# A hybrid diffusion backbone on one core: filler products behind the level batches, and state sums with 64 weight columns

## The chip, the cores and the metric

The kernel runs on one core of one Trainium2 chip. The metric is the device time of one execution in microseconds (us), the median of the runs shown. TensorE runs at one of two clocks, 1.2 or 2.4 GHz; the profile gives the granted share, 0.50 or 1.00.

## The reference, cut to what matters

One trunk layer runs over 256 context and 2048 latent tokens of width 1024: modulation, one input projection, two recurrences, an output projection and an MLP. The change lies in the second recurrence, HGRN2, 8 heads of 64, forward and backward:

```python
def step(s, xs):
    q_c, k_c, v_c, b_c, qd_c, kd_c, fl_c = xs
    diff = b_c[:, :, :, None, :] - b_c[:, :, None, :, :]
    dec = masked_exp(diff, incl)
    a = jnp.einsum('bhid,bhjd,bhijd->bhij', q_c, k_c, dec)
    o = jnp.einsum('bhck,bhkv->bhcv', qd_c, s) + jnp.einsum('bhij,bhjv->bhiv', a, v_c)
    s = fl_c[..., None] * s + jnp.einsum('bhck,bhcv->bhkv', kd_c, v_c)
    return s, o
```

Inside a chunk the attention `a` of a pair (i, j) carries the product of the decays between j and i; the sum over `kd_c` and `v_c` is what the chunk adds to the state.

## The kernel before, in words

The program is a row of phases: front, projection, the first recurrence, a short context phase, the chunk stage (`phase_hgrn_chunks`, line 1764), a phase that scans the states, and the output phases with the MLP. The change touches the chunk stage alone.

The chunk stage works on chunks of C2 = 128 tokens, 16 in all, as 8 periods `j` of two lanes `g` (0 and 1). Partitions 0 to 63 hold the forward direction, 64 to 127 the backward one. The decayed attention is built by doubling: at level `l` (0 to 6) blocks of `1 << l` tokens are joined. For each level and lane:

- TensorE makes a level batch (`level`, lines 2052 and 2053; 32 products, 64 records in the trace, 64 rows by 64 weight columns and 32 moving columns, which fall on the four quarters of the array in turn). Level 6 is `across` (lines 2064 and 2065, two quarters).
- VectorE copies the blocks by mask into `am` (`attend`, 2289) and multiplies the queries by the decay (2309). GpSimd multiplies the keys (2248) and, once per level, makes the next decay products `gg` (`products`, 2229). ScalarE copies half of the keys for the backward side (2162). All of these release the same lane's next level batch.

Between the level batches TensorE's program has other steps of the periods before and after: `tail` (transposes of the keys, 2075 and 2076) at levels 0 and 2, `sums` at levels 1 and 3, `head` (value transposes 2024 and first products 2032) of period j + 1 at levels 4 and 5. `sums` has two parts: the attention times the values (2094, through `values`), and the state sums (2107): for each of 8 heads one product with a 128 by 128 weight tile of `kdt`, whose 128 columns are the two directions of 64, and 64 moving columns. ScalarE evicts the first part; VectorE copies the second into `delta` (2316).

The order on each engine is the order of the loops in its own `body`; TensorE's is unrolled over all periods. At the end of a period ScalarE copies the level 6 result (`b_ax`, 2165) behind its key copy, which waits for GpSimd's level 6; only then may TensorE begin level 0 of the next period. SyncE's queue prefetches with waits on `level_done`. Ahead of the stage `warm_up` issues ten full-array products of constants with 384 columns (2115).

Of the kernel before, what the change touches and what calls it, by code (L numbers as in the profile page):

```python
# [1763 lines left out]
def phase_hgrn_chunks(nc, e):  # L1764

    with nc.cleanup_on_exit(), ExitStack() as ctx:
# [3 lines left out]
        def sem(n):  # L1770
            return nc.alloc_semaphore(name=n)
# [19 lines left out]
        pf, pb = (ctx.enter_context(nc.psum_tensor(f"b_p{n}", [P, 2, HEADS, HD], F32)) for n in "fb")  # L1791
        px = ctx.enter_context(nc.psum_tensor("b_px", [P, 2, HEADS, HD], F32))
        py = ctx.enter_context(nc.psum_tensor("b_py", [P, PAIRS, C2], F32))
        const_in, go, load_go, warm = sem("b_const"), sem("b_go"), sem("b_load_go"), sem("b_warm")
        f_in, k_in, q_in, v_in = ([[e.b_in[n][g], sem(f"b_{n}_in{g}1")] for g in range(2)] for n in "fkqv")
        v_turned, vt_ready, seed, a_seed = sems("v_turned"), sems("vt"), sems("seed"), sems("a_seed")
# [62 lines left out]
        with nc.Block() as block:  # L1859
# [155 lines left out]
            @block.tensor  # L2015
            def _(pe):
                lo, hi = slice(0, HD), slice(HD, P)

                def head(g, i, m):
                    p = m % 2  # L2020
                    pe.wait_ge(v_in[g][p], got(i, m, 16))
                    head_space(pe, g, i, m, vt_ready, d_taken)
                    for a in range(PAIRS):
                        last = nc.tensor.transpose(py[:, a, :], vb[g][p][:, a, :], e.ident)
                    last.then_inc(v_turned[g], 1)
                    pe.wait_ge(km_first[g], at(i, m, 1, 1))
                    pe.wait_ge(q_in[g][p], got(i, m, 32))
                    head_space(pe, g, i, m, a_seed, o_taken)
                    pe.sem_inc(go, 1)
                    for h in range(HEADS):  # L2030
                        for x in (lo, hi):
                            last = nc.tensor.matmul(px[x, 0, h, :], km[g][p][:, h, x], qb[g][p][:, h, x], start=True, stop=True)
                    last.then_inc(seed[g], 1)

                def level(g, i, m, l):
                    p = m % 2
                    if l:
                        pe.wait_ge(q_up[g], at(i, m, L2, l))
                        pe.wait_ge(km_up[g], at(i, m, L2, l))
                        pe.wait_ge(k_up[g], at(i, m, L2, l))  # L2040
                        pe.wait_ge(a_up[g], at(i, m, NA, l))
                    else:
                        pe.wait_ge(q_first[g], at(i, m, 1, 1))
                        if i is not None or m:
                            pe.wait_ge(a_up[g], at(i, m, NA, 0))
                            pe.wait_ge(a_last[g], at(i, m, 1, 0))
                    pe.sem_inc(go, 1)
                    for h in range(HEADS):
                        for x in (lo, hi):
                            ahead = qp[g][p][lo, h, x].rearrange("p (b w s) -> p b w s", w=2, s=1 << l)[:, :, 1, :]  # L2050
                            back = qp[g][p][hi, h, ::-1][:, x].rearrange("p (b w s) -> p b w s", w=2, s=1 << l)[:, :, 0, :]
                            nc.tensor.matmul(pf[x, g, h, 0:HD // 2], ks[g][p][lo, h, x], ahead, start=True, stop=True)
                            last = nc.tensor.matmul(pb[x, g, h, 0:HD // 2], km[g][p][hi, h, x], back, start=True, stop=True)  # L2053
                    last.then_inc(level_done[g], 1)

                def across(g, i, m):
                    p = m % 2
                    pe.wait_ge(q_up[g], at(i, m, L2, NA))
                    pe.wait_ge(km_up[g], at(i, m, L2, NA))
                    pe.wait_ge(k_up[g], at(i, m, L2, NA))  # L2060
                    pe.wait_ge(a_up[g], at(i, m, NA, NA))
                    pe.sem_inc(go, 1)
                    for h in range(HEADS):
                        nc.tensor.matmul(pf[lo, g, h, :], ks[g][p][lo, h, lo], qp[g][p][lo, h, hi], start=True, stop=True)
                        last = nc.tensor.matmul(pf[hi, g, h, :], km[g][p][hi, h, hi], qp[g][p][hi, h, ::-1][:, lo], start=True, stop=True)
                    last.then_inc(level_done[g], 1)

                def tail(g, i, m):
                    p = m % 2
                    pe.wait_ge(k_up[g], at(i, m, L2, L2))  # L2070
                    pe.wait_ge(km_up[g], at(i, m, L2, L2))
                    tail_space(pe, g, i, m, a_seed, o_taken)
                    pe.sem_inc(go, 1)
                    for h in range(HEADS):
                        nc.tensor.transpose(px[:, 0, h, :], ks[g][p][lo, h, :], e.ident[lo, lo])
                        last = nc.tensor.transpose(px[:, 1, h, :], km[g][p][hi, h, :], e.ident[hi, hi])
                    last.then_inc(kt_full[g], 1)

                def sums(g, i, m):
                    p = m % 2  # L2080
                    pe.wait_ge(a_up[g], at(i, m, NA, NA))
                    pe.wait_ge(vt_ready[g], at(i, m, 1, 1))
                    pe.wait_ge(kt_ready[g], at(i, m, 1, 1))
                    pe.sem_inc(go, 1)
                    pz = px[:, :, :, :].rearrange("p x h d -> p x (h d)")

                    def values(t, cross):

                        for a in range(PAIRS):
                            for x in range(2):  # L2090
                                k = slice(x * HD, x * HD + HD)
                                q = 1 - x if cross else x
                                for y in (lo, hi):
                                    last = nc.tensor.matmul(pz[y, q, a * HD:a * HD + HD], vt[g][p][k, a, y], t[k, 2 * a + (y == hi), :],
                                                            start=(a == 0 and not cross), stop=(a == PAIRS - 1 and cross))
                        return last
                    values(am[g][p], False).then_inc(o_half[g], 1)
                    pe.wait_ge(o_half[g], at(i, m, 1, 1))
                    pe.wait_ge(a_last[g], at(i, m, 1, 1))
                    pe.sem_inc(go, 1)  # L2100
                    values(ax[g][p], True).then_inc(o_full[g], 1)
                    tail_space(pe, g, i, m, vt_ready, d_taken)
                    pe.sem_inc(go, 1)
                    new = py[:, :, :].rearrange("p a (y d) -> p (a y) d", y=2)
                    for h in range(HEADS):
                        r = slice(h % 2 * HD, h % 2 * HD + HD)
                        last = nc.tensor.matmul(new[:, h, :], kdt[:, h, :, :].rearrange("p x d -> p (x d)"),
                                                vt[g][p][:, h // 2, r], start=True, stop=True)
                    last.then_inc(d_full[g], 1)

                def warm_up():

                    idle = px[:, :, :, :].rearrange("p x h d -> p x (h d)")[:, 1, 0:3 * P]
                    for _ in range(10):
                        last = nc.tensor.matmul(idle, e.ident, e.cst[:, :, :], start=True, stop=True)
                    last.then_inc(warm, 1)
                    pe.wait_ge(warm, 1)
                    pe.sem_inc(go, 1)

                def first():  # L2120
                    warm_up()
                    for g in range(2):
                        head(g, None, 0)

                def body(i, j, a, c, pre):
                    for l in range(L2):
                        if a:
                            for g in range(2):
                                if l < NA:
                                    level(g, i, j, l)  # L2130
                                else:
                                    across(g, i, j)
                        if c and l in (0, 2):
                            tail(l // 2, i, j - 1)
                        if c and l in (1, 3):
                            sums(l // 2, i, j - 1)
                        if pre and l in (4, 5):
                            head(l - 4, i, j + 1)
                first()
                for j in range(NP + 1):  # L2140
                    body(None, j, j < NP, j > 0, j < NP - 1)
# [1339 lines left out]
```

## Time and profile before

| what | value |
|---|---|
| runs before | 3676.11, 3675.75, 3663.84 us; median 3675.75 |
| the profiled execution | 3675.44 us |
| its span, first to last instruction | 3673.6 us |
| PE busy in the span | 3325.9 us (91%) |
| mean granted clock | 0.922 |
| the chunk stage in the span | from 1645 to 2040 us |

A window's row reads: its stretch from the span's start, its length, then for each engine the busy time and the number of instructions (PE is the matmul side, PEld the weight load), the granted TensorE clock, the busy share of the DMA engines and their GB/s. A timeline row has start, duration, engine, line, operation and the idle time before it with what ended it. An fp32 product leaves two records, a transpose one.

### The profile page before, as it was taken

What the parts mean: (1) busy time and instruction counts of PE and PEld (TensorE: products, weight loads), DVE (VectorE), ACT (ScalarE), POOL (GpSimd) and SP (SyncE); (2) the same over time, 40 slices, a digit from 0 to 9 for tenths busy, and PEclk for the clock granted to TensorE, in tenths of its full rate; (3) what the DMA queues carried; (4) which work ended last, traced back from release to release, by engine and by line L of the source; (5) the groups of instructions that cost most, each with busy time, mean ns of one, the idle gap of its engine ahead of it and who ended that gap; (6) DMA issues with size and microseconds to landing.
All of it is one profiled execution on the core that took longest, in us unless ns stands there. A gap on an engine that the chain in (4) does not pass through costs nothing. (4 is left out here: it accounts for less than half of the span.)

```text
span 3673.6 us, 112919 instructions
## 1 busy us (share of the span) xinstructions
PE 3325.9 (91%) x48215; PEld 2790.8 (76%) x48215; DVE 2083.0 (57%) x3041; ACT 1583.7 (43%) x2345; POOL 1695.8 (46%) x1364
## 2 busy tenths in 40 slices
PE   6799999999978999978888638999999999999998
PEld 3677888888857888877888427878878877787877
DVE  5488610111027888866666676655565556756575
ACT  5566422343214555534444324654454452323243
POOL 0202223333015565626666165456655656656554
PEclk8899999999989999986665669999999999999999
DMA  5133432344233444444331485756656575546453
GB/s 205 50 66 79 98 98 92 107 131 130 73 105 107 129 132 129 134 125 121 105 101 46 158 284 178 259 188 209 208 205 209 178 254 221 219 171 248 165 217 126
DMA packets 458208, 556.25 MB, mean 151 GB/s; under 512 B 120973, under 2 KB 384497, under 8 KB 433529
## 3 DMA queue, kind: packets, MB, share of 16 engines
q1 hardware_dynamic: 431376, 512.93, 43.7%
q10 hardware_dynamic: 20968, 23.28, 1.9%
q0 software_dynamic: 5632, 16.78, 1.6%
q8 instruction: 167, 2.74, 0.3%
q14 instruction: 65, 0.52, 0.0%
HBM read 354.95 MB, written 197.97 MB: 151 GB/s over the span
## 5 line engine op out<-in xcount | busy, mean ns | idle before, releaser
L3147 PE MATMUL o_pg<-o_t_hi,o_s_hi 128*128 128x512 f32 x2016 | 793.6, 394 | 47.9 <-ACT o_part L3194 14.3
L3149 PE MATMUL o_pg<-o_t_lo,o_s_hi 128*128 128x512 f32 x2016 | 789.5, 392 | 0.0
L3150 PE MATMUL o_pg<-o_t_hi,o_s_lo 128*128 128x512 f32 x2016 | 789.2, 391 | 0.0
L600 PE MATMUL p_pg<-h_hi,p_whi 128*128 128x512 f32 (+1 forms) x1384 | 531.9, 384 | 9.6 <-DVE p_wlo L827 9.6
L600 PE MATMUL p_pg<-h_lo,p_whi 128*128 128x512 f32 (+1 forms) x1384 | 519.5, 375 | 0.0
L600 PE MATMUL p_pg<-h_hi,p_wlo 128*128 128x512 f32 (+1 forms) x1384 | 519.3, 375 | 0.0
L3147 PEld LDWEIGHTS o_pg<-o_t_hi,o_s_hi 128*128 128x128 f32 x2016 | 381.1, 189 | 139.0 <-DVE o_s_lo L3354 33.8
L3150 PEld LDWEIGHTS o_pg<-o_t_hi,o_s_lo 128*128 128x128 f32 x2016 | 381.2, 189 | 79.9
L3149 PEld LDWEIGHTS o_pg<-o_t_lo,o_s_hi 128*128 128x128 f32 x2016 | 381.6, 189 | 78.2
L3354 DVE TENSOR_TENSOR o_s_lo<-o_raw,o_s_hi 128x512 fp32r<-128x512 f32 x288 | 267.1, 929 | 197.7 <-ACT o_s_hi L3183 197.6
L600 PEld LDWEIGHTS p_pg<-h_hi,p_whi 128*128 128x128 f32 x1384 | 262.3, 190 | 60.9 <-DVE p_wlo L827 9.8
L600 PEld LDWEIGHTS p_pg<-h_lo,p_whi 128*128 128x128 f32 x1384 | 262.2, 189 | 51.3 <-issue 5.8
L600 PEld LDWEIGHTS p_pg<-h_hi,p_wlo 128*128 128x128 f32 x1384 | 261.9, 189 | 46.8
L3354 DVE TENSOR_TENSOR o_s_lo<-o_mix,o_s_hi 128x512 fp32r<-128x512 f32 x216 | 211.8, 981 | 123.8 <-ACT o_s_hi L3183 123.8
L3183 ACT ACTIVATE o_s_hi<-o_raw 128x512 fp32r<-128x512 f32 x288 | 180.0, 626 | 227.5 <-PE o_pg L3150 216.7
L3080 POOL TENSOR_TENSOR o_xf<-o_xf,o_part 128x512 f32<-128x512 f32 x90 | 158.7, 1764 | 252.2 <-DVE o_part L3344 207.9
L808 ACT ACTIVATE p_y<-p_pg 128x512 f32<-128x512 f32 (+1 forms) x108 | 96.7, 896 | 378.9 <-PE p_pg L600 292.2
L674 POOL TENSOR_SCALAR p_macc<-p_mw,sc 128x512 f32<-128x512 f32 x8 | 13.7, 1708 | 532.9 <-PE p_pg L620 530.8
L3183 ACT ACTIVATE o_s_hi<-o_mix 128x512 fp32r<-128x512 f32 x216 | 135.4, 627 | 213.2 <-PE o_pg L3150 197.8
L3063 POOL TENSOR_TENSOR o_mix<-o_raw 128x512 f32<-128x512 f32 x72 | 101.6, 1411 | 197.8 <-DVE o_s_lo L3354 140.0
L823 DVE TENSOR_TENSOR p_wlo<-p_raw,p_whi 128x1024 fp32r<-128x1024 f32 x37 | 47.1, 1272 | 244.8 <-ACT p_whi L693 241.5
L2053 PE MATMUL b_pb<-b_qp,b_km 64*64 64x32 f32 x3072 | 166.9, 282 | 0.2 <-issue 0.2
(350 smaller groups left out, 6767.1 us busy)
## 6 DMA issues: line engine op xcount, KB each, us to landing
o_raw<-in_w_mlp SPq DMA_DIRECT2D x32, 1024.0 KB, 5.8
scr_f<-o_xf SPq DMA_DIRECT2D x64, 512.0 KB, 7.6
o_raw<-scr_f SPq DMA_DIRECT2D x32, 1024.0 KB, 5.3
scr_w<-o_pre SPq DMA_DIRECT2D x16, 1792.0 KB, 6.8
o_t_raw<-scr_w SPq DMA_DIRECT2D x28, 1024.0 KB, 5.1
o_xf<-scr_x SPq DMA_DIRECT2D x22, 1024.0 KB, 7.8
p_raw<-in_w_in SPq DMA_DIRECT2D x38, 512.0 KB, 5.9
g_kqa<-scr_kqv SPq DMA_DIRECT2D x72, 256.0 KB, 3.0
```

What stands on the lines that cost most here:

```text
L600: last = nc.tensor.matmul(pg[0:m, bank, 0:n], w[:, q, k, 0:m], h[bank][:, k, :], start=(k == 0 and j == 0), stop=(k == KT - 1 and j == 2))
L674: nc.gpsimd.tensor_scalar(macc[:, :], w, sc, None, ALU.mult).then_inc(m_part, 1)
L808: last = nc.scalar.activation(put(yrow[u]), src, f)
L823: dve.tensor_tensor(wlo[:, q, :, 0:m], raw[:, q, :, 0:m], whi[:, q, :, 0:m].bitcast(F32), ALU.subtract).then_inc(w_lo, 1)
L2053: last = nc.tensor.matmul(pb[x, g, h, 0:HD // 2], km[g][p][hi, h, x], back, start=True, stop=True)
L3063: nc.gpsimd.tensor_tensor(mix[:, 0], a21, a22, ALU.add).then_inc(mixed, 1)
L3080: nc.gpsimd.tensor_tensor(t, t, part[:, src], ALU.add).then_inc(x_added, 1)
L3147: nc.tensor.matmul(out, s_hi[:, q, k, :], t_hi[:, q, k, :], start=(not more and k == 0), stop=False, skip_group_check=more)
L3149: nc.tensor.matmul(out, s_hi[:, q, k, :], t_lo[:, q, k, :], start=False, stop=False, skip_group_check=more)
L3150: last = nc.tensor.matmul(out, s_lo[:, q, k, :], t_hi[:, q, k, :], start=False, stop=(k == 3), skip_group_check=more)
L3183: nc.scalar.activation(s_hi[:, q], operand(i, q), ACT.Copy).then_inc(s_hi_ready, 1)
L3354: dve.tensor_tensor(s_lo[:, q], operand(i, q), s_hi[:, q].bitcast(F32), ALU.subtract).then_inc(s_lo_ready, 1)
```

## The change

Three things change in the chunk stage. A tile `pw` of PSUM is added that nothing reads. The state sums of a head become two products with 64 weight columns, one for each direction, that write partitions 0 to 63 and 64 to 127 of the same place. And a product `keep_warm` is issued behind the level batch of lane 0 and once more at the end of each level of `body`, in every period that has level batches: weights are the first 64 rows and columns of the identity, the moving operand 384 columns of constants in 64 partitions, the output goes to `pw`. It waits for nothing and signals nothing.

```diff
--- before.py
+++ after.py
@@ -1791,6 +1791,7 @@
         pf, pb = (ctx.enter_context(nc.psum_tensor(f"b_p{n}", [P, 2, HEADS, HD], F32)) for n in "fb")
         px = ctx.enter_context(nc.psum_tensor("b_px", [P, 2, HEADS, HD], F32))
         py = ctx.enter_context(nc.psum_tensor("b_py", [P, PAIRS, C2], F32))
+        pw = ctx.enter_context(nc.psum_tensor("b_pw", [P, 3, P], F32))
         const_in, go, load_go, warm = sem("b_const"), sem("b_go"), sem("b_load_go"), sem("b_warm")
         f_in, k_in, q_in, v_in = ([[e.b_in[n][g], sem(f"b_{n}_in{g}1")] for g in range(2)] for n in "fkqv")
         v_turned, vt_ready, seed, a_seed = sems("v_turned"), sems("vt"), sems("seed"), sems("a_seed")
@@ -2104,8 +2105,9 @@
                     new = py[:, :, :].rearrange("p a (y d) -> p (a y) d", y=2)
                     for h in range(HEADS):
                         r = slice(h % 2 * HD, h % 2 * HD + HD)
-                        last = nc.tensor.matmul(new[:, h, :], kdt[:, h, :, :].rearrange("p x d -> p (x d)"),
-                                                vt[g][p][:, h // 2, r], start=True, stop=True)
+                        for x in range(2):
+                            last = nc.tensor.matmul(new[x * HD:x * HD + HD, h, :], kdt[:, h, x, :], vt[g][p][:, h // 2, r],
+                                                    start=True, stop=True)
                     last.then_inc(d_full[g], 1)
 
                 def warm_up():
@@ -2116,6 +2118,9 @@
                     last.then_inc(warm, 1)
                     pe.wait_ge(warm, 1)
                     pe.sem_inc(go, 1)
+
+                def keep_warm():
+                    nc.tensor.matmul(pw[lo], e.ident[lo, lo], e.cst[lo, :, :], start=True, stop=True)
 
                 def first():
                     warm_up()
@@ -2130,12 +2135,16 @@
                                     level(g, i, j, l)
                                 else:
                                     across(g, i, j)
+                                if g == 0:
+                                    keep_warm()
                         if c and l in (0, 2):
                             tail(l // 2, i, j - 1)
                         if c and l in (1, 3):
                             sums(l // 2, i, j - 1)
                         if pre and l in (4, 5):
                             head(l - 4, i, j + 1)
+                        if a:
+                            keep_warm()
                 first()
                 for j in range(NP + 1):
                     body(None, j, j < NP, j > 0, j < NP - 1)
```

## Rows read from the trace of the kernel before

**Rows 1.** Windows by period: us; busy (x) of PE, PEld, DVE, ACT, POOL; clock; DMA.

```profile
1661.23:1698.30 37.07, 28.40 (x908) 26.84 (x905) 29.19 (x66) 16.00 (x24) 30.57 (x29) 0.60 0.70 171
...
1839.10:1886.14 47.04, 41.88 (x1096) 39.38 (x1097) 31.13 (x70) 21.93 (x31) 29.72 (x31) 0.60 0.36 103
...
1979.64:2024.60 44.96, 40.06 (x1040) 38.22 (x1040) 25.58 (x66) 18.50 (x26) 24.73 (x30) 0.54 0.13 32
2024.60:2039.62 15.02, 12.78 (x176) 11.79 (x176) 1.38 (x2) 3.58 (x5) 0.00 (x0) 0.50 0.21 53
```

**Rows 2.** Windows, the fifth period cut at levels 2, 4 and 5.

```profile
1839.10:1854.14 15.04, 14.62 (x352) 13.71 (x353) 7.92 (x20) 6.59 (x9) 8.56 (x10) 0.50 0.38 108
1854.14:1868.19 14.05, 13.88 (x354) 13.31 (x353) 7.98 (x22) 7.29 (x9) 6.30 (x8) 0.50 0.41 115
1868.19:1874.71 6.52, 6.52 (x166) 6.01 (x165) 5.72 (x13) 2.27 (x3) 3.85 (x4) 0.50 0.26 76
1874.71:1886.14 11.43, 6.85 (x230) 6.36 (x229) 9.50 (x15) 5.78 (x11) 11.01 (x10) 0.92 0.35 99
```

**Rows 3.** Windows, TensorE fed throughout, one pair of level batches, and the wait at the end.

```profile
1843.30:1874.70 31.40, 31.06 (x742) 29.26 (x740) 19.55 (x50) 14.41 (x19) 17.00 (x19) 0.50 0.41 117
1868.19:1871.76 3.57, 3.57 (x130) 3.51 (x129) 2.83 (x7) 0.42 (x1) 1.07 (x1) 0.50 0.02 5
...
1882.00:1886.14 4.14, 0.00 (x0) 0.03 (x1) 3.13 (x3) 1.26 (x3) 4.14 (x4) 1.00 0.45 127
```

**Rows 4.** Waits in the stage: total us, times, longest us.

```profile
PE b_pf L2052 <- ACT b_ax L2165: 32.7, 7, 4.9
```

**Rows 5.** Timeline of PE, one sums step: start, us, operation.

```profile
1862.22 1.13 PE L2094 MATMUL b_px<-b_am,b_vt 64*64 64x64 f32 x32
1863.52 1.13 PE L2094 MATMUL b_px<-b_ax,b_vt 64*64 64x64 f32 x32 [0.17 <-PE b_px L2094]
1864.58 3.67 PE L2107 MATMUL b_py<-b_vt,b_kdt 128*128 128x64 f32 x16
```

**Rows 6.** Windows, line 2032 alone, at either clock: PE, PEld busy, clock.

```profile
1820.00:1828.75 8.75, 1.98 (x32) 1.79 (x32) 0.50 0.21 62
1828.77:1834.00 5.23, 1.15 (x32) 1.01 (x32) 1.00 0.35 101
```

**Rows 7.** Windows, line 2115 alone, at either clock.

```profile
1646.00:1651.27 5.27, 5.15 (x8) 2.86 (x9) 0.50 0.16 37
1651.27:1655.40 4.13, 4.09 (x13) 2.10 (x11) 1.00 0.00 0
```

**Rows 8.** Windows: ahead of a rise, behind it, and in line 2107.

```profile
1825.35:1828.77 3.42, 3.42 (x78) 2.97 (x77) 3.41 (x4) 2.72 (x3) 3.42 (x4) 0.50 0.42 122
1828.77:1832.18 3.41, 3.41 (x144) 3.13 (x142) 2.83 (x11) 1.72 (x4) 3.41 (x3) 1.00 0.19 57
...
1770.74:1774.16 3.42, 3.42 (x17) 3.42 (x16) 0.00 (x0) 2.71 (x3) 0.00 (x0) 0.50 0.48 135
```

**Rows 9.** Windows of the next stage, lines 2442 (first) and 2432 alone.

```profile
2121.63:2128.82 7.19, 7.19 (x8) 2.49 (x8) 0.50 0.80 309
...
2088.18:2091.59 3.41, 3.41 (x6) 0.55 (x5) 0.50 0.00 0
2091.59:2092.60 1.01, 1.01 (x3) 0.08 (x1) 1.00 0.00 0
```

**Rows 10.** Timeline of POOL, levels 4 to 6 of the fifth period.

```profile
1872.97 1.81 POOL L2229 TENSOR_TENSOR b_gg<-b_gg 128x16 f32<-128x16 f32 x2
1874.74 2.09 POOL L2229 TENSOR_TENSOR b_gg<-b_f 128x512 f32<-128x512 f32 x1
...
1881.04 2.11 POOL L2229 TENSOR_TENSOR b_gg<-b_f 128x512 f32<-128x512 f32 x1
1883.11 2.96 POOL L2248 TENSOR_TENSOR b_k<-b_k,b_gg 128x512 f32<-128x512 f32 x2
```

**Rows 11.** DMA issues of the stage: KB each, us to landing.

```profile
b_ks<-scr_hk SPq DMA_DIRECT2D x16, 256.0 KB, 4.1
```

## The prediction

> **What bounds the kernel now.** I read the stage of the change by period first. Each window runs from one level 0 to the next [rows 1]. A middle period takes 47.04 us: TensorE is busy for 41.88 us of it, VectorE for 31.13 and GpSimd for 29.72, and the granted clock is 0.60. The reader is to see that no engine but TensorE comes near the length, and that TensorE runs mostly at the lower of its two clocks. The first period has no tail or sums and takes 37.07 us, the last one 44.96 us, and 15.02 us of tail and sums follow it.
>
> Next come the windows inside one period [rows 2]. Levels 0 and 1 take 15.04 us and levels 2 and 3 take 14.05 us, both at 0.50 with TensorE full. Level 4 takes 6.52 us, also full. Levels 5 and 6, with the wait for the next period, take 11.43 us at 0.92, with GpSimd busy for 11.01 us. So TensorE at 1.2 GHz sets the first 35.6 us and GpSimd the last 11.4 us.
>
> The third view shows the two ends of this [rows 3]. For 31.40 us TensorE was busy 31.06 us, and the clock was 0.50 all the same. A pair of level batches costs 3.57 us there. At the end of the period it does nothing for 4.14 us, at clock 1.00, and the clock is low again when it resumes. The waits agree: seven times level 0 waited for `b_ax`, 32.7 us in all [rows 4].
>
> **The change part by part.** *The state sums.* Eight products with 128 weight columns take 3.67 us [rows 5]. The new form, 128 rows by 64 weight columns with 64 moving columns, is that of line 2032: 32 records, as many as the sixteen new products will leave, took 1.98 us at 0.50 and 1.15 us at 1.00 [rows 6]. I take 1.7 us off each sums step at the low clock; between the two clocks the bounds are 1.7 and 2.5 us. The Trainium skill, page "TensorE: Matmul & The Clock Gate", section "LDWEIGHTS (loading the stationary operand)", says that a weight load costs by its columns, whatever its rows. By it two loads of 64 columns cost what one of 128 does, the step stays as long, and the time would be some 20 us above my sum. The rows of line 2032 speak against it, since two such products go to different columns of the array and run side by side.
>
> *The filler.* It has the moving columns of line 2115, on a quarter of the array. There a record took 5.15 / 8 = 0.64 us at 0.50 and 4.09 / 12.5 = 0.33 us at 1.00 [rows 7], so a product with its two records costs 1.29 or 0.65 us. Nothing in the trace shows a single quarter at work; the bounds are nothing, if the next batch's other quarters run beside it, and the full price. I take the full price, because the next batch begins with the filler's quarter. There are 14 in a period. Behind each filler the whole next batch is queued, and with it GpSimd, ScalarE and VectorE, who wait for that lane. No other queue is passed, and no wait is added.
>
> *The clock.* This decides. Seven of the stage's nine rises to 1.00 came with `head`. The rows show one: a stretch with `head` at 0.50, then 1.00 [rows 8]. Level batches and tails between them, full as they are, stayed low. So did the sums step whose second half, 17 records in 3.42 us, is line 2107 [rows 8]. The new second half is of the very form that makes up most of `head`, and directly behind 2.4 us of values it makes 4.3 us of dense products, longer than a head's 3 us. I therefore take it that the clock rises near the end of each sums step, at level 1 first. After that TensorE has no pause until level 6, so nothing like the 4.14 us pause ahead of the fall occurs before it.
>
> What the filler itself does to the clock has two bounds. Products with 8 weight rows kept TensorE full for 7.19 us and the clock stayed at 0.50; products with 128 rows and 8 columns were followed by 1.00 [rows 9]. The filler has 64 rows. I take it that it holds the clock but doesn't raise it, between the two.
>
> *The sum for a middle period.* Levels 0 and 1, low until the sums end: 15.04, plus fillers 0.6 (half of the first lies in lane 1's wait), 1.29, 1.29 and 0.65, less 1.7, plus 0.4 for a late rise: 17.5 us. Levels 2 and 3, high: two pairs at an estimated 1.9 us (half of 3.57 and a tail), four fillers at 0.65, the tail 0.55, the sums 2.25, and 0.3 of latency: 9.5 us against 14.05. VectorE's 7.98 us and GpSimd's 6.30 us fit under it. Level 4 to the next period: GpSimd does its level 4, then products of 1.81 and 2.09 us, and later its level 6 of 2.96 us, almost without a pause [rows 10]. Only the first batch comes some 0.95 us sooner, so 17.95 becomes 17.0 us, and the fillers there lie in the time in which GpSimd is late. Then the 4 us pause and the fall remain. Together 44.0 us against 47.04: 3.0 us less, six times: 18 us.
>
> The first period adds eight fillers to levels 0 to 3 at the low clock, 10.3 us. TensorE has 37.07 - 28.40 = 8.7 us of pauses [rows 1], of which 4.8 are the last one; less a little for the rise at its end, it is 6 us longer. The last period with its end gains 2 us net in levels 0 to 3, some 1.6 us in levels 4 to 6, where no head burdens GpSimd, and 3.4 us in the two last sums: 7 us less. Sum: 6 - 18 - 7 = -19. The profiled execution took 3675.44 us (span 3673.6), 0.3 us under the median of the runs. That gives **3656 us**.
>
> **The rivals.** *The filler raises the clock (chance 0.25).* If it counts as the warm-up product did, the rise comes within level 0. Levels 0 and 1 then take about 6.5 + 5.5 = 12 us in place of 17.5, in seven periods, and the first one loses its 6 us: 3656 - 38 - 6 = 3612 us. For it: warm-up products on the same constants were at 1.00 after 5.15 us [rows 7]. Against it: a quarter of the array, and 8 rows did nothing.
>
> *The clock goes as before (0.12).* This one ends slower, and its place is TensorE from level 0 to level 4. Ten fillers at 1.29 us, less 0.7 hidden, less 3.4 us saved in two sums steps, are 8.8 us a period; six of these, 7 us in the first and 8 us in the last give 68 us: 3743 us. It decides once the sums aren't followed by a high clock. For it: TensorE was already full at 0.50 [rows 3], and a filler makes it no fuller. The Trainium skill, the same page, section "Why this matters for your kernels", has it that a busy TensorE, kept so continuously, reaches the full clock. By that, batches without pause would need no filler, and a filler could only cost, as here. The trace disagrees with it: busy 31.06 of 31.40 us at 0.50.
>
> *The rise comes but doesn't hold (0.18).* The level batches let it fall again before level 4. Levels 2 and 3 then save 1.5 us where levels 0 and 1 lose 2.5: 1 us more per period, 7 with the last one, 6 in the first, less 3: 3685 us. A late load would look alike: keys land 4.1 us after their issue [rows 11], which follows level 3's first batch, and ScalarE wants them some 5 us later.
>
> **How the numbers follow.** The forecast has the remaining 0.45, with a range of its own from 3638 to 3675, by the sums' price (1.7 to 2.5 us) and the place of the rise. A half per cent, 18 us, is about what a measurement of this kernel can tell from no change, so the forecast lies just at that edge: 0.25 of its 0.45 go to faster, 0.20 to the same. With the first rival whole, faster has 0.50. The third gives 0.08 to the same and 0.10 to slower, the second all its 0.12 to slower: 0.28 and 0.22. The range of 8 in 10 runs from 3600, under the first rival's time, to 3710, and leaves out the second rival and the far end of the first.
>
> **What would show it.** In the changed profile: the state sums leave 32 records in 2 us or less; the fillers take 1.29 or 0.65 us; the window after each sums step at level 1 has clock 1.00; levels 2 and 3 take under 10 us; level 4 to the next period still takes 17 us, with GpSimd full and a TensorE pause of 3 to 4 us at its end; the stage's mean clock is near 0.8. A clock of 1.00 in level 0 would mean the first rival. A clock of 0.50 from level 0 to level 4 with periods of 56 us would mean the second, and the forecast is then wrong.

## The result, and the profile after

The change made no gain: 3682.6 us (median of 12 runs, 3677.0 to 3697.7) against 3674.65 us for the kernel before (median of 12). The ratio is 1.0025 [1.0016, 1.0034], so it is 0.2% slower, where the prediction said 3656 us. The profiled execution took 3677.04 us, the shortest of the twelve; its span is 3675.2 us.

I read the stage by period first, as in [rows 1]. These are the windows of the changed kernel; columns as there.

```profile
1661.23:1704.03 42.80, 40.25 (x939) 30.41 (x937) 29.09 (x66) 16.06 (x24) 29.67 (x30) 0.64 0.51 139
1704.03:1748.23 44.20, 37.71 (x1160) 29.76 (x1160) 31.76 (x70) 21.96 (x31) 30.24 (x32) 0.87 0.42 116
1748.23:1798.40 50.17, 44.47 (x1156) 34.93 (x1157) 30.93 (x70) 21.92 (x31) 29.74 (x31) 0.74 0.35 97
1798.40:1846.70 48.30, 41.70 (x1158) 33.29 (x1158) 31.73 (x70) 21.96 (x31) 30.23 (x32) 0.78 0.36 101
1846.70:1894.70 48.00, 43.05 (x1160) 34.37 (x1160) 31.00 (x70) 21.98 (x31) 29.80 (x32) 0.75 0.36 101
...
1990.50:2044.02 53.52, 46.13 (x1308) 36.89 (x1308) 26.65 (x68) 22.06 (x30) 23.83 (x30) 0.76 0.17 43
```

The clock rose, from some 0.61 to 0.74 or more in every middle period, and still the middle periods became longer. The six of them take 286.5 us, against 281.3 before and 264 in the forecast. Only the second, with 44.20 us, came as forecast (44.0). The first period (42.80 us, 5.7 more) and the last with its end (53.52 us, 6.5 less) did too: the forecast had 6 more and 7 less. For the last one that is partly luck: nearly all of the gain lies behind level 3, where the forecast had 2 of its 7 us in levels 0 to 3. Over the stage this is 4.4 us more; the span is only 1.6 us longer, so 2.8 us came back outside the stage, in code that is the same.

The next view cuts two of these periods after the sums of level 1 and of level 3, as in [rows 2] (before: 15.04, 14.05 and 17.95 us).

```profile
1798.40:1814.56 16.16, 15.96 (x378) 13.03 (x379) 7.96 (x20) 6.60 (x9) 8.57 (x10) 0.50 0.36 101
1814.56:1829.03 14.47, 11.69 (x382) 9.48 (x381) 7.75 (x22) 6.31 (x9) 6.32 (x8) 0.86 0.39 112
1829.03:1846.70 17.67, 14.05 (x409) 10.78 (x408) 16.02 (x28) 9.05 (x14) 15.34 (x14) 0.98 0.32 92
1846.70:1862.83 16.13, 15.93 (x378) 12.99 (x378) 7.96 (x20) 6.57 (x9) 8.56 (x10) 0.50 0.37 101
1862.83:1873.64 10.81, 9.98 (x382) 8.22 (x380) 7.75 (x22) 5.48 (x8) 6.31 (x8) 0.99 0.50 141
1873.64:1894.70 21.06, 17.14 (x412) 13.16 (x410) 15.29 (x28) 9.93 (x15) 14.93 (x14) 0.82 0.29 82
```

Levels 0 and 1 take 16.1 us, less than the forecast 17.5. In the fourth period levels 2 and 3 are long (14.47 us, TensorE busy for only 11.69) and the rest is short; in the fifth it is the other way round. Means over the six middle periods are 15.2, 13.0 and 19.5 us, where the forecast had 17.5, 9.5 and 17.0. So the loss is behind the first sums step, where I had written that TensorE has no pause until level 6.

The waits say what the pauses are. These are TensorE's waits in the stage (us in total, times, longest).

```profile
PE b_pf L2053 <- ACT b_ax L2174: 20.5, 7, 3.7
PE b_px L2095 <- ACT b_kdt L2189: 7.8, 7, 3.7
PE b_px L2095 <- issue: 5.5, 3, 2.6
PE b_pb L2054 <- issue: 3.2, 4, 1.9
```

The wait for `b_ax` shrank from 32.7 us [rows 4] to 20.5. Grown are the lines with "issue": no other engine, semaphore or transfer that the profile knows ended them. With all over 0.25 us they are 12.8 us in ten places; in the kernel before 2.6 us in four. One of them, in the fifth period, looks like this in the windows (columns as above) and in the timeline (start, us, engine, line, operation, idle time before it in brackets):

```profile
1873.00:1874.12 1.12, 1.12 (x32) 0.89 (x29) 0.27 (x1) 1.10 (x2) 0.00 (x0) 1.00 0.68 198
1874.12:1875.08 0.96, 0.78 (x25) 0.48 (x23) 0.95 (x2) 0.95 (x2) 0.00 (x0) 1.00 0.10 28
1875.08:1876.40 1.32, 0.00 (x1) 0.00 (x1) 0.16 (x1) 0.39 (x1) 0.00 (x0) 1.00 0.00 0
```

```profile
1874.62 0.28 PE L2053 MATMUL b_pf<-b_qp,b_k 64*64 64x32 f32 x2
1876.40 0.19 PE L2053 MATMUL b_pf<-b_qp,b_k 64*64 64x32 f32 x1 [1.50 <-issue]
```

It falls in the middle of level 4's first batch, whose semaphore waits lie all ahead of its first product. At 1876.69 the clock fell, and level 4 and `head` ran at 0.50 until 1883.5. GpSimd, which has to work from level 4 on without a break if the period is to be short, got the first batch late:

```profile
1877.54 1.08 POOL L2257 TENSOR_TENSOR b_k<-b_k,b_gg 128x512 f32<-128x512 f32 x1 [5.32 <-PE b_pb L2054]
1880.37 1.07 POOL L2257 TENSOR_TENSOR b_k<-b_k,b_gg 128x512 f32<-128x512 f32 x1 [1.76 <-PE b_pb L2054]
```

That is how 17.95 us became 21.06. Five of the stage's pauses have a fall of the clock within 2 us behind their end: one each in the third to the sixth period (2.60, 2.07, 1.50 and 1.88 us) and one of 0.87 us in the last. The one of 1.54 us in the second period has none, and that period is the short one.

**Where the pauses come from.** In the list of DMA queues the stage has one that carries instructions. The first row is of the kernel before, the second of the changed one (packets, MB, share of the DMA engines), both over the stage.

```profile
q8 instruction: 69, 1.13, 1.2%
```

```profile
q8 instruction: 73, 1.20, 1.3%
```

1.20 MB in 73 packets are 16 KB each. The periods above sum to 9,202 product and 9,201 weight-load records; at one instruction a record and 256 in a packet these are 71.9 packets. So this is TensorE's own program, which is unrolled over all periods, coming in as it is used. The packet ahead of the pause above began at 1874.12, and TensorE resumed 2.28 us later. I found the same at each of the nine pauses over 0.5 us: the end lies 2.2 to 3.0 us behind the start of such a packet. In the stage of every run below it is 2.2 to 3.1 us. The theory from here on: **at the high clock TensorE uses up 256 instructions faster than they are brought**. A pair of level batches is 128 products' records and 128 weight loads, one packet. At 0.50 it lasts 3.57 us [rows 3], at 1.00 some 2 us.

Two things limit this theory from the start. The packets ahead of the five pauses over 1 us began 4.2 to 6.0 us after the packet before them, so the queue was not at its full rate: what the rows show is a packet that begins too late for the work in hand. And the low clock does not rule such a pause out: the longest one of the kernel before, 1.63 us, fell at 0.50.

### The profile page after: what moved, and what is told of

Its sections match the earlier page's. It is cut to its first block and busy times, and to the rows that moved or that the text cites. A ratio compares the mean times of both kernels' runs of the same rounds, so it can differ in the third digit from the quotient of the medians.

```text
span 3675.2 us, 113879 instructions
## 1 busy us (share of the span) xinstructions
PE 3331.1 (91%) x48695; PEld 2745.5 (75%) x48695; DVE 2084.4 (57%) x3041; ACT 1583.9 (43%) x2345; POOL 1692.6 (46%) x1364
## 5 line engine op out<-in xcount | busy, mean ns | idle before, releaser
L2054 PE MATMUL b_pb<-b_qp,b_km 64*64 64x32 f32 x3072 | 155.8, 253 | 3.2 <-issue 3.2
```

## The experiments

All of them in one table: the median, the ratio to runs of the kernel before beside it (their median was 3671.97 us beside e1 to e4, 3673.4 beside e6 to e11), and from the profiled execution the issue pauses over 0.25 us and the 16-KB packets, from the run's own first level batch to the stage's end. e5 and e12 were executed once and are told by their rows.

| kernel | us | ratio | pauses, us (count) | packets |
|---|---|---|---|---|
| before | 3674.65 | 1 | 2.6 (4) | 69 |
| the change | 3682.60 | 1.0025 [1.0016, 1.0034] | 12.8 (10) | 73 |
| e1 sums only | 3647.92 | 0.9940 [0.9926, 0.9953] | 33.0 (33) | 72 |
| e2 fillers only | 3749.28 | 1.0212 [1.0198, 1.0225] | 6.0 (5) | 71 |
| e3 full-array filler | 3677.46 | 1.0006 [0.9992, 1.0021] | 14.8 (11) | 73 |
| e4 fillers from level 2 | 3661.39 | 0.9979 [0.9964, 0.9993] | 11.2 (9) | 73 |
| e6 filler in six | 3689.66 | 1.0043 [1.0027, 1.0058] | 18.5 (16) | 82 |
| e7 four behind level 6 | 3649.62 | 0.9936 [0.9919, 0.9952] | 31.2 (35) | 72 |
| e8 seven behind level 6 | 3648.41 | 0.9933 [0.9914, 0.9952] | 26.3 (29) | 72 |
| e9 change, joined | 3620.80 | 0.9857 [0.9841, 0.9873] | 3.1 (3) | 49 |
| e10 sums only, joined | 3624.92 | 0.9860 [0.9844, 0.9876] | 10.6 (17) | 48 |
| e11 before, joined | 3644.06 | 0.9917 [0.9901, 0.9934] | 4.5 (3) | 45 |

**The two halves apart.** e1 is the changed kernel without its `keep_warm` calls; e2 is the kernel before with them.

> The change without any filler: only the state sums with 64 weight columns. Two theories. Supply: in the changed kernel TensorE at 2.4 GHz uses up its instructions faster than they are fetched (blocks of 16 KB on the instruction queue, never closer than 3.4 us), stands still for 1.5 to 2.6 us in level 3 or 4, and the clock falls behind that. Thin: the level batches with their filler can't hold the clock, and the pauses are incidental. Here both expect state sums of 2 us at 0.50 and a clock of 1.00 behind many of the sums steps. Supply expects pauses put down to issue only where the clock was high for long, so under 3 us in the whole stage, and periods of 44 to 46 us, 3655 to 3665 us in all. Thin expects the clock to fall within one level of each rise, periods of 46 us and 3668 us.

> The fillers alone, state sums as before with 128 weight columns. Both theories expect no rise behind the sums of level 1, so levels 0 to 4 stay at 0.50 and ten fillers at 1.29 us lie on the path: periods of some 56 us, 3740 us. If the fillers themselves lift the clock, a window in levels 0 to 3 shows 1.00 and the time is under 3700 us.

The state sums alone gain 24 us against the runs beside them. The fillers alone cost 77 us, and on top of the sums 35 us (31 by the ratios). Both theories had expected e1 to be slower than it is (3655 to 3668 us), and its pauses under 3 us where they are 33. By parts, in the six middle periods of the profiled runs, the fillers on top of the sums cost 13.2 us in levels 0 and 1, nothing in levels 2 and 3 (13.0 us in the mean either way) and 8.6 us from level 4 on. One middle period of e1, cut in three and whole:

```profile
1825.40:1838.49 13.09, 12.48 (x372) 11.81 (x375) 8.14 (x20) 6.64 (x9) 8.85 (x10) 0.51 0.44 124
1838.49:1851.45 12.96, 8.97 (x372) 8.23 (x374) 7.65 (x22) 6.33 (x9) 7.11 (x8) 0.89 0.44 125
1851.45:1868.65 17.20, 10.32 (x392) 9.40 (x393) 15.52 (x28) 9.02 (x14) 15.73 (x13) 0.98 0.34 94
1825.40:1868.65 43.25, 31.77 (x1128) 29.44 (x1129) 31.31 (x70) 21.99 (x31) 31.68 (x31) 0.81 0.40 113
```

The clock is 0.89 in levels 2 and 3 without any filler: the sums step at level 1 raises it by itself. TensorE is busy for 8.97 of 12.96 us there. In this period a wait of 2.4 us for VectorE's `b_am` is the longest, with 1.0 us of "issue"; in levels 2 and 3 of all seven periods with sums, "issue" has 14.8 us and all other waits together 7.6. Over the stage:

```profile
PE b_pb L2054 <- issue: 15.3, 15, 2.0
PE b_pf L2053 <- issue: 11.5, 11, 1.9
```

Without the sums the fillers seldom help: in four of e2's six middle periods levels 0 to 3 run at 0.50 to 0.56, in the other two the clock was still high from the period before for a part of them. e2 has periods of 48 to 60 us, as the prediction's second rival has it (its profiled execution, 3723 us, is 26 us shorter than its median):

```profile
1863.72:1923.87 60.15, 58.28 (x1124) 46.11 (x1125) 30.71 (x70) 22.03 (x31) 29.78 (x31) 0.55 0.27 77
```

**What raises the clock.** Two runs ask whether the filler's quarter of the array is too little. e3 makes the filler a full-array product; e5 is a probe in `warm_up`, thirty more products of 384 columns ahead of the ten.

```diff
-                    nc.tensor.matmul(pw[lo], e.ident[lo, lo], e.cst[lo, :, :], start=True, stop=True)
+                    nc.tensor.matmul(pw[:, :, :], e.ident, e.cst[:, :, :], start=True, stop=True)
```

```diff
+                    for _ in range(10):
+                        nc.tensor.matmul(idle[lo], e.ident[lo, lo], e.cst[lo, :, :], start=True, stop=True)
+                    for _ in range(10):
+                        nc.tensor.matmul(idle, e.ident[lo, :], e.cst[lo, :, :], start=True, stop=True)
+                    for _ in range(10):
+                        nc.tensor.matmul(idle[lo], e.ident[:, lo], e.cst[:, :, :], start=True, stop=True)
```

> The change with the filler on the whole array (128 rows, 128 weight columns, the same 384 columns of constants, the same number of instructions). The clock should be 1.00 from level 0 or 1 on, as behind the warm-up products. Supply: then TensorE runs dry in every period, with pauses put down to issue of over 3 us a period (20 us in the stage), and periods don't get under 40 us: 3640 us. Thin: no more pauses than in the changed kernel, periods of 37 us, 3610 us.

> The kernel before, with thirty more products ahead of the ten of the warm-up, on the same constants with 384 columns: ten with 64 rows and 64 weight columns (the filler's quarter), then ten with 64 rows and 128 weight columns, then ten with 128 rows and 64 weight columns. At 0.50 ten take 12.9 us. If the part of the array doesn't matter, the clock rises within the first ten. If rows count and columns don't, it stays at 0.50 through the first twenty, 26 us, and rises in the third ten. If the area counts, none of the thirty lifts it and it rises in the last ten. The time says nothing here: 20 to 38 us longer.

The probe's windows: 64 rows by 64 weight columns, 64 rows by 128, and 128 rows by 64, the last ahead of the rise and behind it.

```profile
1646.21:1659.10 12.89, 12.89 (x20) 4.33 (x20) 4.88 (x4) 2.08 (x2) 2.02 (x2) 0.50 0.08 17
1659.16:1672.10 12.94, 12.94 (x21) 6.49 (x20) 0.00 (x0) 0.00 (x0) 0.00 (x0) 0.50 0.00 0
1672.26:1675.45 3.19, 3.19 (x6) 1.20 (x6) 0.00 (x0) 0.00 (x0) 0.00 (x0) 0.50 0.00 0
1675.45:1678.60 3.15, 3.15 (x11) 1.37 (x10) 0.00 (x0) 0.00 (x0) 0.00 (x0) 1.00 0.00 0
```

Products with 64 rows keep TensorE busy for 25.8 us, whatever their weight columns, and the clock stays at 0.50. With 128 rows it is at 1.00 after 3.2 us. The kinds came in this order only; but 64 rows stayed at 0.50 for longer than all of it in [rows 3], 31.06 us busy of 31.40. So the filler of the change is of a kind that didn't raise the clock, levels 0 and 1 of its first period ran at 0.52, and the first rival is out. A filler with 128 rows isn't enough either: in e3's first period, which has no sums, the clock stayed at 0.50 through levels 0 to 3, with TensorE busy for all of 27.52 us. In e3, whose filler has 128 rows, the clock is 1.00 throughout one period, and it still falls in others:

```profile
1708.10:1751.01 42.91, 36.84 (x1157) 27.21 (x1157) 32.40 (x70) 22.03 (x31) 30.85 (x31) 1.00 0.44 119
...
1841.87:1889.67 47.80, 44.12 (x1157) 32.58 (x1157) 31.34 (x70) 21.98 (x31) 29.77 (x31) 0.82 0.35 99
```

Even a whole period at 1.00 takes 42.91 us, hardly less than e1's 43.25 at 0.81. It has a pause of 2.29 us, and the fillers add to TensorE's work (36.84 us busy against 31.77), so it doesn't say what the clock alone would be worth. Both theories had forecast far less for e3, 3640 and 3610 us.

**Where the fillers cost.** e4 leaves them out in levels 0 and 1, but for the one behind the sums of level 1. e6 keeps them all, and their columns, but issues each as six products of 64 columns, so that 20 more instructions come with each, 280 in a period.

```diff
-                                if g == 0:
+                                if g == 0 and l > 1:
...
-                        if a:
+                        if a and l:
```

> The change with the fillers of level 0 and the one between the two batches of level 1 left out (the one behind level 1's sums stays). Levels 0 and 1 are at 0.50 anyway, so they should get shorter by three fillers less half of the first, 3.2 us a period, 22 us in the stage, and 10 us in the first period for its levels 0 and 1: 3655 us by both theories. Supply adds that TensorE's pauses stay, since the stretch at the high clock begins at the same place; Thin that the clock falls at the same places.

> The change with each filler cut into six products of 64 columns: the same columns, five more products, 20 more instructions each, some 280 a period, 1.1 blocks of 16 KB. Supply expects 8 more fetches in the stage, more and longer pauses put down to issue (over 20 us against 12.8) and 3 us more a period: 3705 us. Thin expects nothing but what the smaller products cost by themselves, 3685 us, and the same pauses.

e4 takes 3661.39 us, 21 of the 35 us back (17 by the ratios): levels 0 and 1 take 13.0 us in the mean where the change had 15.2, 3 us less where the clock is low from the start and the fillers are paid in full. e6 takes 7 us more than the change, though their intervals overlap a little, with 82 packets in place of 73 and 18.5 us of pauses in place of 12.8. The pauses go the way of the theory; the time lies nearer to the 3685 us of its rival than to its own 3705, and the smaller products may cost TensorE time of their own.

**Holding the clock over the end of a period.** e7 and e8 have e1's sums, and four or seven full-array products of constants behind level 6, where TensorE waits anyway.

```diff
+                        if a and l == NA:
+                            for _ in range(4):
+                                keep_warm()
```

> State sums as changed, no filler but four on the whole array behind level 6 of each period, where TensorE waits some 3 to 4 us for the next one. They last 4 x 0.65 us, more where they change the array's shape. Sixteen instructions a period: nothing for the supply. The clock should stay at 1.00 over the end of the period and levels 0 and 1 begin high. Supply: those levels are then bound by the fetch (three blocks, 10 us) in place of 15 us, a period takes 41 us where the sums-only kernel took 43.9, and the pauses grow over its 35 us: 3625 us. Thin: with the clock high nothing bounds them, periods of 38 us, 3605 us.

> The same with seven fillers behind level 6, 4.6 us at the high clock, longer than most waits there. Both theories: the clock holds in every period, and where the fillers outlast the wait they add up to 1 us a period; 3630 us by Supply, 3610 us by Thin.

Their ratios, 0.9936 and 0.9933, can't be told from e1's 0.9940, and both theories had expected 3605 to 3630 us. With seven the clock often stayed at 1.00 over the end of a period (0.83 over the six middle periods, where e1 has 0.74) and fell later in the next one. Again a higher clock brought nothing, with 26.3 us of pauses. But supply is not all that took it: in levels 0 and 1 of the middle periods TensorE waited 4.7 us for "issue" and 11.8 us for other engines, mostly for ScalarE's `b_km` and `b_kdt`.

**Fewer instructions for the same columns.** e11, e10 and e9 are the kernel before, e1 and the change, with one edit more: in levels 0 to 5 the products of two heads become one, with twice the moving columns. The second head's queries then meet the first head's keys, so that part of the attention is another than the reference's. A batch has half its products and half its weight loads.

```diff
-                    for h in range(HEADS):
+                    for h in range(0, HEADS, 2):
...
-                            nc.tensor.matmul(pf[x, g, h, 0:HD // 2], ks[g][p][lo, h, x], ahead, start=True, stop=True)
+                            nc.tensor.matmul(pf[x, g, h:h + 2, 0:HD // 2], ks[g][p][lo, h, x], ahead, start=True, stop=True)
```

> The change with two heads' products joined in the batches of levels 0 to 5: one product with 64 moving columns where there were two with 32. The second head is multiplied by the first head's keys, so that part of the attention is another one. The moving columns are the same, the instructions of a batch half as many (some 770 less a period, 3 blocks of 16 KB of 10), TensorE's time for a batch an estimated 5% less. Supply: hardly a pause put down to issue is left (under 3 us in the stage against 12.8), the clock holds from the first rise to the end of each period, all middle periods take 42 to 44 us as the forecast had it, 3650 us. Thin: the clock falls where it fell, periods stay at 47 to 48 us less 1 us for the batches, 3675 us.

> The same joining in the kernel with the state sums alone. That kernel had 35.4 us of pauses put down to issue in the stage, in 34 places. Supply: under 4 us are left, and periods get to 38 to 40 us from 43.9: 3615 us. Thin: the pauses stay where TensorE waits for its data, periods 43 us, 3642 us.

> The same joining in the kernel before. There TensorE ran at 0.50 where the batches are, and a pair took 3.57 us, about as long as the fetch of the 256 instructions that it is made of. Both theories: the batches take 5% less, 1 us a period, 3666 us; more only if the clock rises at other places too. This is the measure of what joining does by itself.

The joined change takes 3620.8 us, its stage has 49 packets and three pauses. One middle period of e9:

```profile
1809.62:1849.12 39.50, 31.20 (x772) 22.60 (x773) 31.81 (x70) 21.98 (x31) 31.49 (x31) 0.90 0.43 122
```

The joining itself helps the kernel before by 29 us, which I had expected to be 8: it also takes TensorE time away at the low clock. What counts is what the change does on either base. Unjoined it costs 8 us; joined it gains 23 us (3644.06 to 3620.80), where the prediction had 19. In the profiled runs a middle period has 3.1 us less, where the prediction had 3.0; e9's profiled execution is 11 us shorter than its median. The fillers on top of the sums cost 35 us unjoined and nothing that can be told joined (3624.92 to 3620.80, with intervals that overlap). That fits a supply that is short in one case and not in the other; it does not prove it. TensorE's own work shrinks as well, and then fillers lie in its waits for the other engines: in e10's fifth period it is busy for 28.44 of 40.89 us and only 1.4 us of the rest are "issue".

**The supply by itself.** So the last run measures it with nothing else around: the kernel before, with sixteen rounds of 256 instructions and one full-array product added behind `warm_up`. There are no waits and no semaphores between them.

```diff
+                    for _ in range(16):
+                        for n in range(64):
+                            x, y = (lo, hi)[n // 2 % 2], (lo, hi)[n % 2]
+                            nc.tensor.matmul((pf, pb)[n % 2][x, 0, 0, 0:16], e.ident[y, y], e.cst[y, 0, 0:16], start=True, stop=True)
+                        last = nc.tensor.matmul(idle, e.ident, e.cst[:, :, :], start=True, stop=True)
```

> Kernel before, with a stream added behind the ten products of warm_up: sixteen rounds of 64 quarter-array products of constants with 16 moving columns (the four quarters in turn; 128 records and 128 weight loads, so 256 instructions a round, one block of 16 KB) and one full-array product with 384 columns, which is there to keep the clock at 1.00. It computes nothing that is used. By the level batches of the changed kernel (64 records, with their weight loads, in 1.13 us at 1.00) a round takes at most 2.26 + 0.65 = 2.9 us, 46 us for all sixteen. Theory (TensorE's instructions arrive at most one block in some 3.2 to 3.4 us): the rounds take 3.3 to 3.5 us each once what was stored is used up, 50 to 56 us for all, with idle time that waits for nothing (issue) of about 0.5 us or more in most rounds, ended 2.2 to 3.0 us after the start of a fetch, and fetches 3.2 to 3.5 us apart. Rival (the pauses of the stage come from its waits and semaphores, not from the supply): the rounds take 2.9 us or less, without a pause, and fetches come closer together than 3.2 us. If the clock is 0.50 there, a round takes about 3.6 + 1.3 us and the run tells nothing.

The windows show the run of rounds, then one stretch between pauses, the pause behind it, and the stretch from a packet's start to the resumption. Below them stand TensorE's waits and the queue of instructions over the sixteen rounds.

```profile
1656.80:1710.80 54.00, 46.79 (x1956) 36.44 (x1952) 0.00 (x0) 0.00 (x0) 0.00 (x0) 1.00 0.02 5
1663.01:1666.01 3.00, 3.00 (x128) 2.34 (x128) 0.00 (x0) 0.00 (x0) 0.00 (x0) 1.00 0.02 5
1666.01:1666.46 0.45, 0.01 (x2) 0.00 (x0) 0.00 (x0) 0.00 (x0) 0.00 (x0) 1.00 0.00 0
...
1664.12:1666.46 2.34, 1.90 (x103) 1.60 (x102) 0.00 (x0) 0.00 (x0) 0.00 (x0) 1.00 0.03 7
```

```profile
PE b_pf L2119 <- issue: 3.7, 7, 0.7
PE b_pb L2119 <- issue: 3.4, 7, 0.6
```

```profile
q8 instruction: 16, 0.26, 2.0%
```

The clock is 1.00 throughout, no other engine and no other queue is at work, and still TensorE stops fourteen times, for 0.35 to 0.72 us, once a packet. Its work between two stops is 3.0 to 3.1 us, a little over the 2.9 expected. A packet begins about 1.1 us after the last pause and TensorE resumes 2.3 to 2.7 us after that. The fifteen spacings between packets are 3.41 to 3.75 us, 3.55 in the mean (1657.19 to 1710.42). So pauses come without any wait or semaphore, and the rival that puts them down to the stage's waits alone is out. That waits make them longer, up to the 2.6 us of the stage, is not excluded: here none is over 0.72 us. In this stream 256 unrolled instructions take about 3.5 us. That packets could come faster with more demand isn't seen in any run; the closest pair of all is 3.20 us apart, in e1. This is one execution.

## Why the prediction was wrong

The step that failed is the sentence "After that TensorE has no pause until level 6", and with it the term of 9.5 us for levels 2 and 3 and the 17.0 us from level 4 on. They measured 13.0 and 19.5 us in the mean. The sum counted TensorE's work, VectorE's, GpSimd's and the transfers of data, and left out what feeds TensorE its program. That is not the whole miss, though. By part of a period:

- **Levels 2 and 3, TensorE's own work**: the fifth period took 10.81 us without a single issue pause, with two packets begun in it. The pairs with their fillers came as forecast (3.34 us for 3.2). The sums step did not: 2.94 us at 1.00 for a term of 2.25 (2.64 in the sixth period), with a wait of 0.56 us for ScalarE's `b_kdt` ahead of it where 0.3 stood. So 9.5 us were about 1 us short before any pause. The wait and the sums step, and the packets over the 10.81 us:

```profile
1870.14:1870.70 0.56, 0.00 (x1) 0.04 (x1) 0.56 (x5) 0.54 (x2) 0.43 (x1) 1.00 0.94 265
1870.70:1873.64 2.94, 2.66 (x100) 2.34 (x100) 1.22 (x2) 1.90 (x4) 1.51 (x3) 1.00 0.85 242
```

```profile
q8 instruction: 2, 0.03, 1.4%
```

- **Levels 2 and 3, pauses**: 1.54, 2.60 and 2.07 us in the second, third and fourth period, 0.52 in the sixth. In the seventh the clock was low, and they took 17.05 us.
- **From level 4 on**: the third, fifth and sixth period, at 20.9 to 21.5 us, have the clock at 0.50 during level 4, behind a pause. The fourth met a pause of 2.07 us too, but had the clock back before level 4, and took 17.7.

All pauses of the six periods are 11.9 us, of a miss of 22.5 (286.5 for 264). The rest lies with the low clock and the sums step, less the 2.3 us a period that levels 0 and 1 gave back.

Point by point:
- **The state sums**: right. 32 records take 1.97 us at 0.50 and 1.15 us at 1.00, as [rows 6] had it, against 3.67 us. The two loads of 64 columns do not cost what one of 128 does. The windows of line 2109 alone, at either clock (busy of PE and PEld, clock):

```profile
1840.00:1862.85 22.85, 1.97 (x32) 1.79 (x32) 0.63 0.35 97
1866.00:1874.00 8.00, 1.15 (x32) 1.01 (x32) 1.00 0.69 196
```

- **The filler's price**: right. A pair of batches with two fillers takes 6.07 us at 0.50, where it had 3.57 without: 1.25 us each, for the 1.29 of the forecast. At 1.00 it takes 3.34 us, the second row.

```profile
1852.54:1858.61 6.07, 6.07 (x141) 4.49 (x143) 3.11 (x7) 3.44 (x4) 3.56 (x4) 0.50 0.60 164
1866.80:1870.14 3.34, 3.34 (x136) 2.69 (x132) 2.65 (x9) 2.41 (x3) 2.77 (x4) 1.00 0.57 162
```

- **The clock rises with the sums step at level 1**: right in six of seven periods. Why, is open: e5 shows that products with 128 rows can raise it where 64 rows did not, but the sums of the kernel before have 128 rows too and ran at 0.50 [rows 8]. In the seventh period the clock was still high from before, fell within the values, and the state sums, broken by a pause of 0.74 us, didn't raise it. Levels 2 and 3 then ran low, with TensorE full and every filler at its full price:

```profile
1955.77:1972.82 17.05, 16.85 (x381) 13.16 (x381) 8.01 (x22) 5.96 (x8) 6.29 (x8) 0.52 0.23 65
```

- **The filler holds the clock**: at most a little. Over the six middle periods the change has 11 falls and a mean clock of 0.78, e1 without fillers 16 falls and 0.74. The clock stayed high over four pauses of supply (1.54, 0.59, 0.52 and 0.47 us) and fell behind five (2.60, 2.07, 1.88, 1.50 and 0.87 us). What the filler adds to the clock doesn't show in the time.
- **Levels 0 and 1**: 15.2 us in the mean, better than 17.5, since two of the six (13.5 and 12.9 us) began with the high clock left from the period before; the other four took 16.1 or 16.2.
- **Level 4 to the next period**: 17.65 us in two periods, near the forecast 17.0; 18.5 to 21.5 us in the other four, three of them with the low clock in level 4.
- **The rivals**: the time is that of the third (3685 us), "the rise comes but doesn't hold". It named the level batches as what lets the clock fall. The trace puts pauses of supply ahead of five of the falls, and the batches are what uses up instructions fastest. That its time fits is luck: against the kernel before, levels 0 and 1 are 0.2 us longer a period (2.5 in the rival), levels 2 and 3 are 1.0 shorter (1.5), and level 4 on is 1.6 longer, where the rival had no loss.

The Trainium skill, page "Runtime: NRT & Kernel Launch", section "Instruction fetch mechanics", says that the instructions come in blocks of 16 KB, 256 at a time, the next one fetched while this one runs, and that the cost of a crossing is mostly hidden. The first half agrees with the packets here. The second holds for the kernel before, whose stage is mostly at the low clock (2.6 us of pauses in 378), and not at the high one, where e12 pays 0.35 to 0.72 us a block and the small products of e1 up to 2.0 us.

Two things stay open. Why some pauses are longer than e12's: in the stage the packet starts only 0.8 us ahead of the pause (1874.12 and 1874.90), in e12 1.9 us, and no view says what holds it. In e12 the packets begin every 260 records of TensorE, which is one round; between 1868.14 and 1874.12 there are 364, so this one began late by count as well. And what takes the clock away: a pause of 1.54 us in the second period left it at 1.00 where one of 1.50 us in the fifth and one of 0.87 in the last did not, and in the seventh it fell with no pause of supply ahead.

## What to carry to other kernels

Before a stretch of small products is sped up, by the clock or otherwise, count its instructions: in an unrolled program of this kernel 256 of them (products and weight loads together) took about 3.5 us in a stream of their own, and no two packets of any run began closer than 3.20 us. Where the work behind them takes less, a faster TensorE waits, and in this stage the clock fell behind half of these waits. Count fillers at their price at the low clock, too: in levels 0 and 1 it was paid nearly in full. Then fewer and wider products are worth more than a fuller array; here the state sums alone (0.6% faster) are the version to keep, and the fillers should go.

## What the runs showed of the hardware

- With 384 moving columns, the rows of the array told the clock here, and not its columns: 20 products with 64 rows, 25.8 us without a pause, left it at 0.50; with 128 rows and 64 weight columns it was at 1.00 in 3.2 us. It isn't all: the state sums of the kernel before have 128 rows and ran at 0.50 for 3.42 us [rows 8].
- A pause of instruction supply has a sign in the trace: TensorE's idle time is put down to "issue" and ends 2.2 to 3.1 us behind the start of a 16-KB packet, in the chunk stage of every run here.
- A looped stage has no supply at all to pay. In the first recurrence, at clock 1.00, 100 us hold 5,480 product and 5,476 weight-load records, 43 packets' worth (window of the changed kernel), and over 400 us of it (1200 to 1600) the list of queues has no row for instructions:

```profile
1300.00:1400.00 100.00, 91.22 (x5480) 86.18 (x5476) 84.16 (x166) 53.47 (x87) 60.85 (x72) 1.00 0.44 130
```

```profile
## 3 DMA queue, kind: packets, MB, share of 16 engines
q1 hardware_dynamic: 70656, 53.24, 44.5%
```

That runs at 256 instructions in 2.3 us over 100 us, where no two packets of the unrolled stages began closer than 3.20 us. One pass of this loop (line 1396) takes 14.03 us and has 768 products' and 769 weight-load records, six packets' worth. It suggests that the chunk stage, written as a loop, could have the change's gain; that wasn't tried. The section of the Trainium skill named above says that there is no cache of instructions, and that a taken branch whose target lies outside the current window of two blocks forces a fetch; this loop is six blocks long, and its rows show no fetch in 400 us.
